# Expert feed-forward layer: one expert at a time in four column quarters, turns on VectorE, down weights in 8 KB runs

## The reference

```python
logits = (xt @ w_router + b_router)            # xt: normed rows, 512 x 1024
top_val, top_idx = lax.top_k(logits, 4)
gates = jax.nn.softmax(top_val, axis=-1)
...
def expert_block(args):
    tok, g, e = args
    xb = xt[tok]                               # rows of this expert's tokens
    hb = clamped_swiglu(xb @ w_gu[e] + b_gu[e])    # w_gu[e]: 1024 x 2048 (gate, up)
    yb = hb @ w_down[e] + b_down[e]                # w_down[e]: 1024 x 1024
    return yb * g[:, None].astype(yb.dtype)

def clamped_swiglu(gu):
    gate, up = gu[..., :D_EXPERT], gu[..., D_EXPERT:]
    gate = jnp.minimum(gate, 7.0)
    up = jnp.clip(up, -7.0, 7.0)
    return (up + 1.0) * gate * jax.nn.sigmoid(1.702 * gate)
```

## Time and profile before

| | us |
|---|---|
| median of 3 runs (2745.76 to 2748.36) | 2746.55 |
| the profiled execution's own time | 2733.44 |
| its span, first to last instruction | 2731.6 |
| PE busy, whole span | 2548.1 (93%) |
| VectorE busy | 933.4 (34%) |
| ScalarE busy | 701.4 (26%) |
| GpSimd busy | 136.8 (5%) |
| matmuls of gate and up, L1261 (6144 records) | 695.2 |
| matmuls of down, L1288 (3072 records) | 344.5 |

### The profile page before, as it was taken

The page is one execution under the profiler, slowest core; times in us unless marked ns, Lnnn a source line. Parts: engine busy times, 40 slices in busy tenths (PEclk is TensorE's granted clock), DMA queues, the critical chain, the costliest instruction groups (busy, mean ns, idle before and its releaser), DMA issues. The chain is left out here.

```text
span 2731.6 us, 49644 instructions
## 1 busy us (share of the span) xinstructions
PE 2548.1 (93%) x21426; PEld 1501.2 (55%) x21426; DVE 933.4 (34%) x1449; ACT 701.4 (26%) x1275; POOL 136.8 (5%) x110
## 2 busy tenths in 40 slices
PE   8989987999999999999999789879888799899998
PEld 6658754333333333333333258656677677788887
DVE  5575253111111111111111153547645434422233
ACT  4353331000000000000000142347555223422222
POOL 0003000000000000000000010001122000000000
PEclk9989998999999999999999989999999899999999
DMA  5343223999999999999999743421100323122220
GB/s 209 116 167 128 104 83 124 401 408 406 396 393 391 393 389 394 391 390 391 389 395 394 269 162 110 169 96 54 50 4 4 136 89 139 47 93 93 103 98 31
DMA packets 115976, 587.00 MB, mean 215 GB/s; under 512 B 12640, under 2 KB 14432, under 8 KB 71200
## 3 DMA queue, kind: packets, MB, share of 16 engines
q1 hardware_dynamic: 98944, 539.07, 51.1%
q10 hardware_dynamic: 11008, 24.98, 2.5%
q0 software_dynamic: 5888, 20.97, 2.2%
HBM read 564.00 MB, written 20.97 MB: 214 GB/s over the span
## 5 line engine op out<-in xcount | busy, mean ns | idle before, releaser
L1261 PE MATMUL psum<-weight_ring,expert_xT 128*32 128x512 f32 x3120 | 347.8, 597 | 1.5 <-ACT expert_xT L1344 1.5
L1261 PE MATMUL psum<-more_weights,expert_xT 128*32 128x512 f32 x3024 | 347.4, 593 | 0.0
L368 DVE TENSOR_TENSOR w_low<-weight_ring,w_high 128x2048 fp32r<-128x2048 f32 (+1 forms) x92 | 213.4, 2321 | 322.6 <-ACT w_high L363 322.2
L363 ACT CAST w_high<-weight_ring 128x2048 fp32r<-128x2048 f32 (+1 forms) x88 | 166.6, 1893 | 290.5 <-PE psum L402 144.2
L1261 PEld LDWEIGHTS psum<-weight_ring,expert_xT 128*32 128x32 f32 x3120 | 99.0, 110 | 221.2 <-issue 220.8
L1402 DVE TENSOR_SCALAR gate<-psum 128x512 f32<-128x512 f32 x48 | 33.2, 692 | 540.8 <-PE psum L1268 540.8
L1261 PEld LDWEIGHTS psum<-more_weights,expert_xT 128*32 128x32 f32 x3024 | 95.5, 110 | 196.7 <-issue 190.0
L1288 PE MATMUL psum<-more_weights,expert_hT 128*32 128x512 f32 x1584 | 178.7, 594 | 0.0
L1350 ACT COPY expert_hT<-psum 128x512 f32<-128x512 f32 x48 | 28.0, 586 | 537.1 <-PE psum L1225 511.6
L1288 PE MATMUL psum<-weight_ring,expert_hT 128*32 128x512 f32 x1488 | 165.8, 594 | 0.0
L402 PE MATMUL psum<-mix_hT_high,w_high 128*128 128x512 f32 x384 | 156.0, 406 | 6.5 <-PEq L1981 3.5
(11 more groups left out here) (540 smaller groups left out, 4040.9 us busy)
## 6 DMA issues: line engine op xcount, KB each, us to landing
weight_ring<-in_w_gu SPq DMA_DIRECT2D x130, 1024.0 KB, 8.3
more_weights<-in_w_gu SPq DMA_DIRECT2D x126, 1024.0 KB, 7.0
more_weights<-in_w_down SPq DMA_DIRECT2D x66, 1024.0 KB, 10.1
weight_ring<-in_w_down SPq DMA_DIRECT2D x62, 1024.0 KB, 9.2
weight_ring<-in_w_in SPq DMA_DIRECT2D x35, 1024.0 KB, 5.1
weight_ring<-in_w_ada SPq DMA_DIRECT2D x24, 1024.0 KB, 4.8
weight_ring<-in_w_ffn_in SPq DMA_DIRECT2D x22, 1024.0 KB, 4.8
expert_table<-expert_y ACTq DMA_DIRECT2D x64, 192.0 KB
```

What stands on the lines that cost most here:

```text
L363: self.m.nc.scalar.copy(high, w).then_inc(self.rounded.sem, 1)
L368: self.m.nc.vector.tensor_tensor(low, w, high.bitcast(F32), ALU.subtract).then_inc(self.ready.sem, 1)
L1261: ins = T.matmul(ps[NR * up + j][quarter(q), :], xT[:, k, i, quarter(j)], w[i][:, up * D + c * 512:up * D + (c + 1) * 512], start=(k == 0) ...
```

## The change

- One expert at a time, 32 steps. A column quarter q now stands for a quarter of the expert's output columns (`QD` = 256). A gate/up matmul still has 512 columns: 256 of gate and 256 of up, read as eight runs of 64 columns (`inner_quarters`), into banks 0 to 2. A down matmul has 256 columns, into banks 3 to 5.
- x is gathered as quarter rows: `hidden` is seen as 2048 rows of 1 KB, an index is 4 times the token plus the quarter, and three gathers of 128 rows fill the 128 partitions. `moe_entry` writes the normed rows in an order of columns that fits, and loads the router's weights in the same order with eight DMAs instead of one.
- x and h are turned by VectorE in 32 x 32 blocks (`V.transpose`) straight into `xT` and `hT`. PE's transpositions and ScalarE's copies go.
- VectorE's clamps and products take a whole expert at once, 768 elements; y is copied in one piece and stored in 1 KB runs, four DMAs per expert.
- Down weights: partition p holds rows 2p and 2p + 1, one run of 8 KB.
- One list per step covers 128 entries with twelve short matmuls; marking ranks is three operations per expert.
- The overflow loop in `moe_exit` gets a copy that undoes the order of columns.

Its core:

```diff
 def gate_up_units(dram, e):
-    return [dram["w_gu"][e(i), k * P:(k + 1) * P, :] for k in range(GUN) for i in range(EG)]
+    return [dram["w_gu"][e, k * P:(k + 1) * P, :] for k in range(GUN)]
...
+def unit_rows(z):
+    if len(z.shape) == 3:
+        return z.rearrange("a p n -> p (a n)") if z.shape[-1] == SLOT else z.rearrange("a (p r) n -> p (a r n)", r=2)
+    return z if z.shape[-1] == SLOT else z.rearrange("(p r) n -> p (r n)", r=2)
+def inner_quarters(z):
+    return z.rearrange("p (k q c) -> p k q c", q=NQ, c=2 * ROUND)
+def by_quarters(z):
+    return z.rearrange("p (k q c) -> p k q c", q=NQ, c=ROUND)
+def mark_ranks(nc, oc, iota, members, e):
+    for j in range(NR):
+        last = nc.vector.tensor_tensor(oc[:, :, j, :].rearrange("p t (q i) -> p t q i", q=NQ),
+                                       iota[:, ROUND * j:ROUND * j + ROUND].unsqueeze(1).unsqueeze(1).to_broadcast([P, NT, NQ, ROUND]),
+                                       members[:, :, e].unsqueeze(3).to_broadcast([P, NT, NQ, ROUND]), ALU.is_equal)
+    return last
+def list_rows(nc, bank, oc, tok):
+    for j in range(NR):
+        for t in range(NT):
+            last = nc.tensor.matmul(bank[:, 2 * j:2 * j + 2], oc[:, t, j, :], tok[:, 2 * t:2 * t + 2], start=(t == 0), stop=(t == NT - 1))
+    return last
...
             def gather():
-                for i in range(EG):
-                    nc.gpsimd.indirect_dma_start(x[i][:, :], None, hidden, bass.IndirectOffsetOnAxis(ap=ix[0:CAP, i:i + 1], axis=0)
-                                                 ).then_inc(gathered[i].sem, 16)
+                for j in range(NR):
+                    nc.gpsimd.indirect_dma_start(x[:, j, :], None, hidden, bass.IndirectOffsetOnAxis(ap=ix[:, j:j + 1], axis=0)
+                                                 ).then_inc(gathered[j].sem, 16)
...
+            def gate_up(n0, e, loop=None, half_way=lambda: None):
                 for k in range(GUN):
+                    w = inner_quarters(landed(n0 + k, loop))
+                    if k == 2:
+                        half_way()
...
+                    for j in range(NR):
                         if k == 0:
+                            pe.wait_ge(x_ready.sem, e * NR + x_ready.at(j + 1))
+                            if j == 0 and loop is not None:
+                                pe.wait_ge(gate_ready.sem, loop + gate_ready.at(0))
+                                pe.wait_ge(gu_freed.sem, loop + gu_freed.at(0))
+                        for q in range(NQ):
+                            ins = T.matmul(ps[j][part(q), :], xT[:, j, k, :], w[:, :, q, :], start=(k == 0), stop=False)
+                            if j == 0 and q == 0:
+                                release(ins, n0 + k)
...
+            def down(n0, e, loop=None):
+                for k in range(DNN):
+                    w = landed(n0 + k, loop)
+                    for r in range(2):
+                        for j in range(NR):
+                            if k == 0 and r == 0:
+                                pe.wait_ge(h_ready.sem, e * NR + h_ready.at(j + 1))
+                                if j == 0 and not (isinstance(e, int) and e == 0):
+                                    pe.wait_ge(y_copied.sem, e + y_copied.at(0))
+                            for q in range(NQ):
+                                ins = T.matmul(y_banks[part(q), j, :], hT[:, j, 2 * k + r, :], w[:, r * D + q * QD:r * D + (q + 1) * QD],
+                                               start=(k == 0 and r == 0), stop=(k == DNN - 1 and r == 1))
...
+            gate_up(0, 0, half_way=lambda: make_list(0))
+            gate_up(GUN, 1, 1, lambda: make_list(1))
+            down(GUN + GUN, 0)
+            with pe.Fori(2, LAST) as e:
+                gate_up(GUN, e, e, lambda: make_list(e))
+                down(GUN + GUN, e - 1, e)
+            gate_up(GUN, LAST, LAST)
+            down(GUN + GUN, LAST - 1, LAST)
+            down(N - DNN, LAST)
...
+            def turn_x(e):
                 for j in range(NR):
+                    dve.wait_ge(gathered[j].sem, e * 16 + gathered[j].at(16))
+                    V.transpose(xT[:, j, :, :].rearrange("p k s -> p (k s)"), x[:, j, :]).then_inc(x_ready.sem, 1)
+            def leave_banks(e):
...
+                dve.wait_ge(gu_done.sem, e + gu_done.at(1))
+                V.tensor_scalar(g[:, :, :], gate_up_banks[:, :, 0:QD], 7.0, None, ALU.min).then_inc(gate_ready.sem, 1)
+                V.tensor_scalar(u[:, :, :], gate_up_banks[:, :, QD:2 * QD], 7.0, -7.0, ALU.min, ALU.max).then_inc(gu_freed.sem, 1)
...
+            def turn_h(e):
+                dve.wait_ge(h_step.sem, e + h_step.at(1))
                 for j in range(NR):
+                    V.transpose(hT[:, j, :, :].rearrange("p (k r) s -> p k r s", r=2),
+                                u[:, j, :].rearrange("p (k s r) -> p k r s", k=DNN, r=2)).then_inc(h_ready.sem, 1)
...
             with dve.Fori(1, LAST) as e:
+                next_index(e)
+                marks(bass.ds(e + 2, 1))
+                leave_banks(e)
+                turn_x(e + 1)
+                mark(bass.ds(e + 1, 1))
                 swiglu(e)
+                copy_y(e - 1)
+                turn_h(e)
```

More of the change, by code:

```diff
@@ L62 @@
 DNN = 4
-GROUPS = E // EG
 EXTRA = 6
@@ L1168, in _, with load @@
         def _(sp):
-            def load(n, src, late=0):
-                if n >= SLOTS:
-                    sp.wait_ge(ring.used, late + U0 + n - SLOTS + 1)
+            def load(n, src, late=None):
+                if late is not None or n >= SLOTS:
+                    sp.wait_ge(ring.used, U0 + n - SLOTS + 1 if late is None else late + U0 + n - SLOTS + 1)
                 elif n < NSLOT:
                     sp.wait_ge(ring.used, U0 + n - NSLOT + 1)
[L1175 to L1186, removed]
+                src = unit_rows(src)
+                sp.dma_start(slot(n), src).then_inc(landing(n)[0], 16)
+            for n in range(ring.next_load - U0, GUN + LOOP):
+                load(n, raw[n])
+            with sp.Fori(2, E) as e:
+                for q, src in enumerate(gate_up_units(m.dram, bass.ds(e, 1)) + down_units(m.dram, bass.ds(e - 1, 1))):
+                    load(GUN + q, src, (e - 1) * LOOP)
+            for n in range(N - DNN, N):
+                load(n, raw[n])
             ring.next_load = ring.next_use = U0 + N
@@ L1414, in copy_y @@
-            def copy_y(group, e=None):
-                for j in range(NR):
-                    dve.wait_ge(down_done.sem, group * NR + down_done.at(j + 1))
-                    if j == 0 and e is not None:
-                        dve.wait_ge(y_stored.sem, group * 64 + y_stored.at(0))
-                    V.tensor_copy(y[:, j, :], ps[j][:, :]).then_inc(y_copied.sem, 1)
-            dve.sem_inc(y_copied.sem, NR)
-            dve.sem_inc(y_stored.sem, 1)
-            mark(slice(0, EG))
-            mark_ranks(slice(EG, 2 * EG))
@@ L3528, in _ @@
             pe.wait_ge(onehot.sem, onehot.at(1))
-            for i in range(EG):
-                for t in range(NT):
-                    last = T.matmul(ps[5][0:CAP, 2 * i:2 * i + 2], oc[:, t, i, :], tok[:, 2 * t:2 * t + 2], start=(t == 0), stop=(t == NT - 1))
-            last.then_inc(listed.sem, 1)
+            list_rows(nc, ps[5], oc, tok).then_inc(listed.sem, 1)
         @block.scalar
@@ L3593, in _ @@
             V.memset(members[:, :, E:E + 2], 0.0)
+            for q in range(NQ):
+                V.memset(quarter[ROUND * q:ROUND * q + ROUND, :], float(q))
             def copy_turned(t):
@@ L3758, in plan @@
     units += tiled("w_ckv", 0, 4) + wide("w_ckv", 4, 8) + tiled("w_cq", 0, 4) + wide("w_co", 0, 4)
[L3759 to L3764 removed]
+    units += [unit_rows(z) for z in expert_units(dram)]
     units += tiled("w_in_2", 0, 9) + tiled("w_ada", 12, 24) + [dram["w_in_2"][u] for u in RWKV_UNITS]
```

330 lines of the change are left out of this document (113 added, 217 removed).

## The result

| | before | after |
|---|---|---|
| median, us | 2746.16 (4 runs) | 2669.32 (4 runs, 2664.05 to 2677.49) |
| profiled execution | 2733.44 | 2664.34 |
| its span | 2731.6 | 2662.5 |
| period of one expert | 34.18 | 32.13 |

The ratio is 0.9726, 95% interval [0.9692, 0.9759]: 77 us less by the medians, 69 between the two profiled executions. The forecast was 2700 with a range from 2680; the kernel is faster than the range allowed.

A forecast was written before the change was run, and what follows sets the result against it. PE was taken to bound the expert stage before, the transfers after. Stage 48 us less, entry +2, exit unchanged: -46 us, profiled execution 2733.4 to 2687, median 13 us above it at 2700; range 2680 to 2765.

The forecast's parts named there:

- the sum of the transfers: Expert stage: weights, y and x need 33.0 us of transfer per expert after the change, against 33.5 before.
- terms for y and x: Expert-stage transfers: y stores 1.5 us and x gathers 1.5 us per expert, at 64 ns per 1 KB packet.
- the entry: Before the expert stage: marks, list, index, scaling and eight router loads make it grow by 2 us.
- PE's sum: Expert stage: PE needs 32.4 us per expert after the change, against 34.18 before.
- rival (3): Gate and up: PE reads the weight runs at 1 us more per expert; -21 us, 2726; chance 0.05.
- rival (4): Down: 32-wide tiles' weight loads stand open, 110 ns per set; +116 us, 2863; chance 0.03.
- VectorE hidden: Expert stage: VectorE's 10.4 us per expert hide under PE's 32.4, except single stands of 2.6 and 1.7 us.
- I take 1507.5: End of expert stage: transfers end near 1508, PE alone at 1500; 1507.5 taken, 48 us less.
- The exit does not change: After the expert stage: the exit takes as long as before, no gain or loss.
- (1): Gather of x: drag stays per packet, 221 ns, transfers 36.8 us per expert; +73 us, 2820; chance 0.13.
- (2): Gather of x: drag goes by bytes, 89 ns, 33.6 us per expert; -28 us, 2719; chance 0.12.
- (5): Expert stage: PE becomes free but transfers still bind at the old 34.2; no change, 2747; chance 0.07.

The follow-up runs named there:

- the pairs: The changed kernel with weight slots given back two at a time, as before the change: 0.9741, 2673.9 us.
- PE work put back: The changed kernel with three groups of four unread 128x128 PE transpositions added per expert during gate and up: 1.0018, 2744.2 us.
- before with more loads: The kernel before with 512 KB more to load per expert, into a tile nobody reads: 1.0022.

## Why the prediction was wrong, by its own steps

The direction was right, and so was PE's part: it was the limit before, and its work per expert came out nearly as summed. The step that failed is the sum of the transfers, by its terms for y and x: 3.0 us per expert forecast, 1.8 measured. It made the transfers the limit after the change, and they are not: PE still is. As a size this is 7.5 of the 31 us by which 2700 was too high; the others are PE's smaller sum (6.4), the entry (1.6), the exit (7.6) and the step to the median (8), all to the same side. The range went down to 2680 and left no room for them together.

- **PE's sum, 32.4 us per expert: nearly right, 32.14.** Gate and up 20.6 forecast, 20.6 measured (48 sets at 10.30/24, from 529.13 to 539.43); bias 0.7, 0.65; down 10.3, 10.36; the list 0.8, 0.53 (what 518.30 to 539.43, 21.13 us, holds beside the 20.6). A down set takes (545.26 - 540.08)/24 = 0.216 us. The strided read costs nothing (10.30/24 = 0.429): rival (3) fell, and rival (4) with the down sets. The Trainium skill, "TensorE: Matmul & The Clock Gate", section "Part 3: Packing small matmuls — row/col tiling", lets a weight load overlap running matmuls only when its row group differs; with all tiles in the same rows, and twice the loads per column, the down of one expert took 10.36 us: the measurement decides against it for such tiles.
- **VectorE hidden: right.** Its stands are 2.4 us at the second expert and 1.48 at the end (2.6 and 1.7 forecast). Three block transpositions took 1.09 us, 0.36 each against 0.45. (The lower end, 0.27, isn't what its two rows give: 473 ns for 512 elements are 0.24 us for 256. Nothing hangs on it.)
- **The transfers, "Sum 33.0 us": the step that failed.** They need 31.72. Weights were sized well (30.0; the 12.58 MB at 421 GB/s are 29.9), y and x were not: 3.0 us forecast, 1.8 left. The queues after, 560 to 1400 us (all packets, then packets, MB, share of each queue):

```profile
DMA packets 61336, 353.09 MB, mean 420 GB/s; under 512 B 8048, under 2 KB 18214, under 8 KB 20803
q1 hardware_dynamic: 45604, 332.07, 94.8%
q10 hardware_dynamic: 11862, 10.42, 3.6%
q0 software_dynamic: 3870, 10.61, 3.2%
```

  By packet time x takes 0.032 x 32.13 = 1.03 us per expert and y 1.16, against 1.5 each. The rows of x did not stay 1 KB packets. Between 2 and 8 KB there are 20803 - 18214 = 2589 packets, and only x can have them (weights go in 8 KB, y in 1 KB): 10.61 MB in 2589 are 4.1 KB each, four rows to a packet, a quarter as many packets as were counted; the other packets of q0 are under 512 B. And packet times add up to 101.6% of the time, so they are no sum of costs. The whole 13.37 MB per expert in 31.72 us are 421 GB/s, the rate of the weights alone: x and y cost their bytes, and no drag is left to see. The same way of counting had made 33.5 of the 32.77 that the kernel before needs.
- **"I take 1507.5" (the transfers end the stage): wrong by that.** PE ended it, at 1494.0. Of the 15.5 us between 1507.5 + 2 and 1494.0, 7.5 are the step from the transfers to PE, 6.4 PE's own smaller sum, 1.6 the entry (+0.4 instead of +2).
- **"The exit does not change": wrong by 7.6 us,** 3.2 in the way there (shown by the pairs) and 4.4 in the exit's first steps. For the second the cause is not shown. PE's wait ahead of the bias of down was 7.37 us before, named issue, and 2.99 after, named the load of that bias; with PE work put back it was 7.40 again, with the change in place:

```profile
1580.61 3.78 PE L1547 MATMUL psum<-exit_b_down,exit_gates_T 32*128 32x512 f32 x8 [7.40 <-issue]
```

  The load itself landed at most 3.9 us after its issue before and 4.4 after, so it is not what takes 7.4; and as the long wait came back with the change in place, it doesn't belong to one of the two kernels. What the traces show is a load of instructions (queue q8, 16 KB) inside the wait, 4.5 to 5 us after its start, in before (1566.8 to 1574.1 us) and with PE work put back (1573.3 to 1580.6):

```profile
q8 instruction: 1, 0.02, 1.1%
```

```profile
q8 instruction: 1, 0.02, 0.8%
```

  The third kernel with a long wait here, before with more loads (6.89 us), has one in it too; the eleven others, with 2.1 to 3.0 us, have none. That PE waits for these instructions fits all fourteen, but no run moved that load. If it is so, the 4.4 us are luck of where a program's instruction loads fall, and no gain of the change.
- **The step from the profiled execution to the median.** 23 of the 31 us by which 2700 was too high are in the points above. The other 8: the profiled execution of before lay 13 us under its median, that of after 5.
- **Rivals (1), (2), (5): fell.** Weights and gather together went at 414 GB/s, the weight packets at 0.704 x 70.4 us / 156 = 318 ns each (882 to 886.4 us) and not 445 as in the earlier trace rows; the period is 32.13.

Where the gain came from: the stage's 62 us are 32 x 2.05 = 65.6, less 3.6 (beside its 32 periods the stage holds 6.2 us now and held 2.6). With the transfers of before, 32.77, PE's saving could have been had down to that, 32 x 1.41 = 45 us; the other 0.64 us per expert, at most 20 us, needed cheaper transfers too. At most, because twelve slots hide a shortage for a while: with 512 KB more to load they hid about 9 us of it over the stage (20.0 instead of 29), so some 11 of the 20 are left as an estimate. Both changes of the transfers in the kernel before give 0.22 + 0.48 = 0.70 (0.32 + 0.55 by the lines); the 128-row form is the larger part. In the kernel before it moves a third more of 4 KB rows, 0.13 MB or 0.31 us at 421 GB/s, which the changed kernel does not; 0.70 + 0.31 = 1.01, near the 1.05 between the two kernels. These sums are worked out from single profiled executions; PE's part of the change with the old transfers was not run.

No run points to a version that beats the changed kernel by more than can be told: the transfers leave 0.41 us per expert, 13 us, and the two smaller pieces of PE work, the list (0.53) and the bias (0.65), were not moved elsewhere in any run.

## What to carry to other kernels

Where two resources both read full, make a kernel with less work on one of them: the period that is left is the other's need, and it told here at once what packet times had mis-sized by 1.3 us. A share of 1.02 is no sign of a limit reached: it read the same with the transfers waited for and with 1% to spare; the trend of the time from issue to landing over the stage tells the two apart. Small traffic beside a large stream was sized best by its bytes at the stream's rate here, with a surcharge only for the form that was seen to drag. And a period that jitters is read with a line through all its marks, not off two of them.

## What the runs showed of the hardware

- Beside weights that go at 421 GB/s, a gather of 96 rows brings the 16 engines together down while it runs (315 and 335 GB/s with 4 KB rows, 372 with 1 KB rows); one of 128 rows hardly does (422 and 414).
- Rows of 1 KB gathered into 128 partitions move in packets of 4 KB, four rows each (10.61 MB in 2589 packets, after).
- One fp32 transposition of 128x128 between matmuls takes 0.26 us of PE, four take 0.59: each further one 0.11.
- Reading the weights in 8 runs of 64 columns or 16 of 32 costs PE nothing (0.429 us per set of 512 columns).
